# Weight slots moved to a multiple of 512 bytes, and one expert's down weights loaded as nine transfers

## The reference

```python
g_sel = argmax(t @ w_rg + b_rg)                       # 4 groups of 8 experts
top_p, top_i = top_k(softmax(e_logits of the group), 2)
for gi in range(4):                                   # 32 experts
    hg = einsum('td,edf->tef', t, w_gate[sl])         # 1024 x 512 each
    hu = einsum('td,edf->tef', t, w_up[sl])
    act = silu(hg) * hu * weights[:, sl, None]
    out = out + einsum('tef,efd->td', act, w_down[sl])  # 512 x 1024 each
```

## Time and profile before

| | |
|---|---|
| median of 3 runs | 1198.58 us (1197.28 to 1199.71) |
| the profiled execution | 1195.88 us |
| its span, first to last instruction | 1194.2 us |
| mean granted TensorE clock, share of full speed | 0.904 |
| PE busy, share of the span | 933.3 us, 78% |
| DVE busy | 353.7 us, 30% |
| ACT busy | 203.0 us, 17% |
| moved by DMA | 436.17 MB, mean 365 GB/s |
| DMA queue q1 (SyncE's), share of 16 engines' span | 87.8% |
| chain that ended last | PE 48%, DMA 36%, issue 5%, DVE 5% |

### The profile page before, as it was taken

The page is one execution under the profiler, slowest core; times in us unless marked ns, Lnnn a source line. Parts: engine busy times, 40 slices in busy tenths (PEclk is TensorE's granted clock), DMA queues, the critical chain, the costliest instruction groups (busy, mean ns, idle before and its releaser), DMA issues.

```text
span 1194.2 us, 26453 instructions
## 1 busy us (share of the span) xinstructions
PE 933.3 (78%) x11004; PEld 593.6 (50%) x11004; DVE 353.7 (30%) x1161; ACT 203.0 (17%) x600; POOL 8.0 (1%) x24
## 2 busy tenths in 40 slices
PE   7999989667668786796799998986667666665854
PEld 6887755334334443453388777443334333333532
DVE  4656352111112222132155654321111111111213
ACT  2366211000001010010024652110000000000001
POOL 2000000000000000000000000000000000000000
PEclk9998989888789998998899999898787888888988
DMA  9853389999999999999997235899999999999995
GB/s 328 313 234 142 109 337 426 426 426 426 426 425 423 426 426 425 401 423 428 409 374 312 82 131 232 349 424 426 427 426 426 427 426 426 428 423 427 425 425 215
DMA packets 50633, 436.17 MB, mean 365 GB/s; under 512 B 9408, under 2 KB 13760, under 8 KB 24640
## 3 DMA queue, kind: packets, MB, share of 16 engines
q1 hardware_dynamic: 50496, 434.26, 87.8%
HBM read 433.20 MB, written 1.05 MB: 364 GB/s over the span
## 4 chain that ended last, share of the span: by engine, by line
PE 48%; DMA 36%; issue 5%; DVE 5%; SPq 3%; DVEq 2%; ACT 1%; another core or an unknown queue 0%; ACTq 0%
DMA ring<-in_w_up 32%; PE ps L622 14%; PE ps L710 7%; PE ps L638 5%; PE ps L853 5%; DMA ring<-in_w_down 3%; PE ps L647 3%; PE ps L590 3%; PE ps L726 2%; SPq L461 1%; PE ps L610 1%; PE ps L715 1%; SPq L463 1%; DMA ring<-in_w_in 1%; PE ps L822 1%
## 5 line engine op out<-in xcount | busy, mean ns | idle before, releaser
L622 PE MATMUL ps<-ring,xg 128*32 128x256 f32 x4352 | 319.8, 457 | 174.5 <-DMA ring<-in_w_up 166.6
L622 PEld LDWEIGHTS ps<-ring,xg 128*32 128x32 f32 x4352 | 173.0, 131 | 304.5 <-issue 245.2
L1203 DVE SCALAR_TENSOR_TENSOR th<-th,ps 128x128 f32<-128x128 f32 x72 | 20.7, 288 | 592.3 <-ACT th L975 592.3
L638 PE MATMUL ps<-ring,actT 128*32 128x256 f32 x2304 | 139.5, 382 | 14.2 <-issue 12.9
L975 ACT ACTIVATE th<-ps 128x128 f32<-128x128 f32 x72 | 20.0, 278 | 514.9 <-PE ps L622 480.1
L638 PEld LDWEIGHTS ps<-ring,actT 128*32 128x32 f32 x2304 | 68.9, 109 | 75.6 <-DVE actT L1207 22.6
L590 PE MATMUL ps<-xh,Pb 128*32 128x256 f32 x1152 | 80.7, 397 | 24.5 <-issue 21.3
L710 PE MATMUL ps<-hT,ring 128*128 128x256 f32 x416 | 93.3, 381 | 1.3 <-ACT hT L1012 0.8
L710 PEld LDWEIGHTS ps<-hT,ring 128*128 128x128 f32 x416 | 78.0, 190 | 14.6 <-issue 4.0
L647 PE MATMUL ps<-ysb,PwT 32*128 32x256 f32 x992 | 71.5, 402 | 0.0
L590 PEld LDWEIGHTS ps<-xh,Pb 128*32 128x32 f32 x1152 | 39.4, 113 | 49.1 <-issue 26.0
(11 more groups left out here) (259 smaller groups left out, 690.0 us busy)
## 6 DMA issues: line engine op xcount, KB each, us to landing
ring<-in_w_down SPq DMA_DIRECT2D x62, 2048.0 KB, 41.0
ring<-in_w_gate SPq DMA_DIRECT2D x60, 2048.0 KB, 45.0
ring<-in_w_up SPq DMA_DIRECT2D x60, 2048.0 KB, 46.5
ring<-in_w_in SPq DMA_DIRECT2D x6, 2048.0 KB, 16.5
ring<-in_w_out SPq DMA_DIRECT2D x4, 2048.0 KB, 19.6
ring<-in_w_gate SPq DMA_DIRECT2D x8, 1024.0 KB, 30.0
ring<-in_w_up SPq DMA_DIRECT2D x8, 1024.0 KB, 31.7
ring<-in_w_in SPq DMA_DIRECT2D x6, 1024.0 KB, 16.4
```

The lines of the kernel that those rows point to most:

```text
L622: last = mm(b_gate[j * SLOTS:(j + 1) * SLOTS, 0:2 * GQ], tokens[:, k, :], ring[:, low:high + 1:high - low, o:o + GQ], start=(k == 0), stop ...
L638: last = mm(b_y[j * SLOTS:(j + 1) * SLOTS, 0:DQ], actT[:, c * SLOTS:(c + 1) * SLOTS], ring[:, slot, o:o + DQ], start=(c == 0), stop=(c == ...
```

## The change

The ring starts at the next multiple of 512 bytes: byte 34,816 in place of 34,496, 320 more, and with it everything that lies behind it. The room is there. The down weights of expert 16 are loaded, in each layer, as eight transfers of 8 partitions each (partitions 64 to 127) followed by one of 64 partitions (0 to 63), in place of one of 128. The slot's semaphore counts nine transfers for it, and TensorE waits for all nine. No other instruction changes.

```diff
@@ -65,6 +65,7 @@
 SUM_ORDER = (0, 2, 3, 1)
+EIGHTS = NE // 2
@@ -182,7 +183,7 @@
-TRANSFERS = {c: len(W_IN_PIECES[c[2]]) if c[1] == "in" else 2 if c[1] in ("front", "back") else 1 for c in ALL}
+TRANSFERS = {c: len(W_IN_PIECES[c[2]]) if c[1] == "in" else 2 if c[1] in ("front", "back") else 1 + P // 16 if c[1:] == ("down", EIGHTS) else 1 for c in ALL}
@@ -283,6 +284,7 @@
         more = sb("more", [1, 2 * NE + 1], I32)
 
 
+        base[0] = -(-base[0] // 512) * 512
         ring = sb("ring", [P, RING + LATE, CHUNK])
@@ -448,6 +450,10 @@
                 elif part == "down":
                     src = w_down[li, n, :, :].rearrange("(p c) d -> p (c d)", c=FC)
+                    if n == EIGHTS:
+                        for r in range(P // 2, P, 8):
+                            sp_.dma_start(to[r:r + 8, :], src[r:r + 8, :]).then_inc(signal, 16)
+                        to, src = to[0:P // 2, :], src[0:P // 2, :]
                     if n == NE - 1:
```

## The result

The changed kernel takes 1218.16 us (median of 4 runs, 1217.42 to 1218.62), the kernel before, timed beside it, 1199.14 us (4 runs, 1197.28 to 1200.20). The ratio is 1.0163, with a 95% interval from 1.0147 to 1.0179: slower by 1.6%. The forecast was 1200.8 us, with a range up to 1204.5; the result lies above it.

What follows compares the result with a forecast made beforehand. The prediction took the transfer rate to pace three stretches, 665.3 us, with the latest DMA engine deciding. Slots -1.1 and expert 16's loads +3.3 gave +2.2 us on the median of 1198.58: 1200.8 us, range 1193.8 to 1204.5.

Steps and rivals of the forecast that it cites:

- Expert 16's down weights: Splitting this load in both layers unbalances the DMA engines: 2.4 us in layer 1, 0.9 in layer 0, +3.3 us in all.
- Added by the 64: 4 rows on each: In the split load, the 64-row transfer gives each of sixteen engines 4 rows, replacing 8 rows removed from every engine.
- the bound of 2.46 us: Per layer: eights all on the same eight engines give these 12 rows, the others 4, plus and minus 4 x 0.615 us.
- The upper bound, 4.9 us over both layers: The split load's most costly case: eights at full cost in both layers, always on the same eight engines.
- The late-engine term: At layer 1's end, nine engines run late; the eights load at least one of them further, taken as 2.4 us.
- The flat stretch at nine: Tail after the last load: the DMA share at nine engines would vanish, leaving one or two alone some 2 us more.
- "In layer 0 ... it shows only at 590": Layer 0's load lands where TensorE sets the pace, so its imbalance shows only at 590 us; 0.9 us, bounds 0 and 2.46.
- Slots: Slots moved to a multiple of 512 save 1 ns a row on the transfer-paced stretches, 1.1 us; upper bound 11 us.
- Rival 1: Alignment pays on every row of the 665.3 us: at 7 ns a row 7.6 us gained, 1194.3 us; chance 0.22.
- SyncE and the waits: Sixteen more issues, 0.33 us each unhindered, 2.6 us more a layer, covered by 49 us from issue to landing: no cost.
- rival 3: Small transfers fill the DMA queue and engines run dry up to 4.9 us in layer 1, dip near 950: 1205.7 us; chance 0.08.
- Rivals 2 and 4: Eights dealt round all engines, nothing moves: 1197.5 us, chance 0.15; the one late engine late only when profiled: 1194.1, 0.06.

Runs made afterwards that it cites:

- f4_offset256: Against the kernel before: slots start 256 bytes past a multiple of 512, expert 16's down weights still one transfer; 1191.10 us, ratio 0.9932.
- e1_align: Against the kernel before: slots start on a multiple of 512, expert 16's down weights still one transfer; 1191.84 us, ratio 0.9952.
- f2_halves: Against e1_align: expert 16's down weights as two transfers of 64 neighbouring partitions; 1208.74 us, ratio 1.0082 to the kernel before.
- e3_columns: Against e1_align: expert 16's down weights as eight transfers of all 128 rows, 2 KB of each; 1192.44 us, ratio 0.9949 to the kernel before.
- e4_spread: Against the changed kernel: each transfer of eight takes every fourth partition within 64 to 127, then the 64; 1214.02 us, ratio 1.0137 to the kernel before.
- f1_home: Against e4_spread: the spread eights go to partitions 0 to 63, the 64 to the upper half; 1210.26 us, ratio 1.0094 to the kernel before.

## Why the prediction was wrong

**The failed step** is in *Expert 16's down weights*: "Added by the 64: 4 rows on each", and the bound of 2.46 us that was worked out from it. It priced a row at 0.615 us wherever it goes in SBUF, and asked only which engine carries it. The upper bound, 4.9 us over both layers, was no bound. The runs showed in its place that a row's price doubles, from 0.61 to 1.27 us, when the rows at work go to one half of the partitions, and that this holds up the loads around it too: 10.9 us in layer 0 and 11.5 in layer 1, where 0.9 and 2.4 were forecast. The forecast had neither this case nor a rival for it. The trace before shows no weight transfer to fewer than 128 partitions. The prediction saw that this left an unknown and named it ("What the trace cannot show is which"), but took it for a question of engines alone.

**The size, step by step.** In layer 1 the changed kernel's expert part is 13.7 us longer than f4_offset256's (445.6 against 431.9). The 22 slow slices above add up to 4,491 GB/s us where 429 each would be 9,438, so they lose 22 - 4491/429 = 11.5 us. Most of the rest is the tail, shown here from 1150 to 1215 us in 40 slices of 1.625 us, for e1_align, f2_halves and the changed kernel:

```profile
GB/s 403 413 454 403 413 434 418 413 429 303 257 247 197 45 0 0 25 280 38 0 18 418 209 0 0 0 0 0 0 0 0 0 0 0 0 0 0 0 0 0
```

```profile
GB/s 434 403 454 434 413 444 434 423 434 444 413 403 439 413 429 413 423 429 418 418 429 282 247 237 187 20 0 10 134 189 10 0 179 421 45 0 0 0 0 0
```

```profile
GB/s 413 444 423 423 454 403 423 444 434 423 434 444 413 434 444 398 439 413 398 439 429 418 429 423 373 363 358 166 86 81 50 5 0 10 161 171 0 0 272 373
```

e1_align ends with 303, 257, 247, 197, 45, the nine engines of the earlier trace rows, and so does f2_halves. The changed kernel has 373, 363, 358 (13 or 14 engines) and then 166, 86, 81, 50, three engines alone for some 4 us. In lost time, the sum of (428 - GB/s)/428 x 1.625 over the slices named, that is 5.8 us against 4.1; by slices of 0.25 us it is 5.6 against 3.7. By those finer slices all four kernels with eights lose 5.4 to 6.1 us in the tail, and the eight kernels with slots on a multiple of 256 that load expert 16 without eights 3.5 to 3.8. **The late-engine term was real and cost 1.6 to 1.9 us in layer 1, where 2.4 were forecast.** The flat stretch at nine is gone and a few engines stay alone, as the text said would be seen, though three for 4 us and not one or two for 2. f2_halves, without eights, keeps the old tail.

**"In layer 0 ... it shows only at 590"** was wrong. The dip there is 21 us at a mean of 206, which loses 10.9 us, and the part is 444.1 - 433.6 = 10.5 us longer. TensorE's lead over the transfers hid next to nothing of it; the queue's 49 us from issue to landing are no cover for a fall in the rate, since every load behind is late by as much. The prediction read off the chain that TensorE sets the pace from 319 to 494 us, but the DMA share was 1.00 at 423 GB/s there as well. The one pause of the queue, near 492 us, is worth 1.9 us at full rate, and a pause of some 2 us stands in the changed kernel too, near 505: there was no slack for 10.9 us to go into.

**Slots.** The mechanism of the bytes ahead of a boundary was given 1 ns a row, since packets of 4 bytes take 8.1 ns and "have no second piece". Measured are 7,864 rows for 7,810 in 300 us, 614.6 - 610.4 = 4.2 ns. Over the 1,088 rows that is 4.6 us; the two expert parts of e1_align are 2.8 and 2.4 us shorter than before, 5.2. The median gained 6.6 us, and where the other 1.4 lies these rows don't tell: the mixer parts vary by more from one profile to the next (the experts begin at 160.02 us in e1_align's, at 163.33 in f4_offset256's). Rival 1, at 7 ns and -7.6 us, was nearer than the forecast. The error was to take what a 4-byte packet takes for the fixed part of a 16 KB row. They need not be the same thing, and the difference of two row lengths had left 10 ns, a proper bound, with no row that told how it divides.

The beats of the Trainium skill ("DMA: Bandwidth & Descriptors", section "How a descriptor splits into AXI transactions") had the boundary right: any multiple of 256 pays. They had the size wrong: 518 beats for 512 would be 1.2%, measured was 0.7%, and 64, with 514 beats, cost as much as 192.

**SyncE and the waits** held in the main. Its nine issues in layer 1, and the gate and up behind them:

```profile
920.91 6.36 SPq L455 DMA_DIRECT2D ring<-in_w_down  x8
927.32 1.16 SPq L469 DMA_DIRECT2D ring<-in_w_down  x1
928.52 3.00 SPq L469 DMA_DIRECT2D ring<-in_w_gate  x1
931.57 4.81 SPq L469 DMA_DIRECT2D ring<-in_w_up  x1
```

Eight take 6.4 us, 0.8 each where 0.33 was said, and they don't wait 4.23 us apiece. There is a dip near 960 us, close to the mark of rival 3, but its cause is another: e3_columns has eight transfers and no loss, and f2_halves has the dip with two. A mark that two mechanisms share decides nothing between them.

**Rivals 2 and 4** fell: the tail changed its shape, and to the bad side. The sum for the changed kernel, in place of -1.1 + 3.3, is -6.6 for the slots, and for the loads 10.9 + 11.5 of dips and 1.6 to 1.9 of tail, 24.0 to 24.3 of the 26.3 measured.

## What to carry to other kernels

Cut a load along its columns, or into odd and even partitions, and not into parts that each stay in one half of the partitions (0 to 63 or 64 to 127). The first two were free here in a queue that never empties, and one 2 MB load in two halves cost 8.4 us, the time of 1.7 full loads. Eights taken from every fourth partition of a half cost 22 us over both layers as well, so it is not neighbours alone. Ask of every transfer which partitions it reaches as well as which engines carry it, and when a bound rests on one side of a transfer only, name the other side as unknown. Start large buffers on a multiple of 256 bytes; that alone gave 1191.10 to 1191.84 us, less than both kernels, and no cut of expert 16's load went measurably below it.

## What the runs showed of the hardware, and what stays open

- Sixteen busy engines can move half the bytes: at shares of 1.01 to 1.09 the changed kernel moved 195 to 233 GB/s (360 to 380 us). The DMA share alone doesn't tell a full rate; the share beside the GB/s does.
- A slow load slows its neighbours. Two halves hold 2 MB, which at half rate take 9.8 us in place of 4.9; in the queue of layer 1 the low rate lasted 16 slices (8.0 us lost), 3.4 MB in all, so about 1.3 MB of whole transfers before and behind went slowly too. That engines several us apart mix a half with whole loads, and the whole loads' rows wait at the crowded ways, would give this; it is argued, and no run separates it.
- With the 64 rows behind them in the lower half, neighbouring eights, spread eights and sixteens lie within 7.6 us of each other in the kernel (1218.16, 1214.02, 1210.52), though alone their rates are 66 to 74, 188 to 197 and 139 to 180 GB/s. The 64 behind them may run beside them, in the other half's ways; that is argued, not measured. Why the spread eights cost 3.8 us more in the upper half with the 64 in the lower (e4_spread) than the other way round (f1_home) is open.
- Whether the ways lie on SBUF's side or HBM's is not separated by a run; the same cuts from rows of HBM that lie otherwise would tell.
- A starved TensorE came back slower: in the dip of layer 0 it was busy 1.6 to 2.3 us of each 4 from 368 to 380 us, and its granted clock was 0.69 at 368 to 372 us and 0.50, its lower level of 1.2 GHz, at 380 to 384; in e1_align it was 1.00 from 350 to 388, with the engine busy 32.5 of 38 us. What that cost beside the wait itself was not measured.
- 64 and 192 bytes past a boundary cost the same 4 ns a row of 16 KB, and 256 nothing. Whether shorter rows pay as much each was not tried.
